# Swapping the two halves of a 128-token block for the expert dots: a pair of DMAs in place of identity matmuls

## The reference

```python
def reference(x_prompt, x_sample, ...):
    # for the prompt, then (with states and caches) for the samples
    q, k, v, g, qs, ks, vs = split(rms_norm(x, norm1_g) @ w_in)     # 2816 columns
    o_ret = retention(rotate(q), rotate(k), v)                      # 4 heads of 128, blocks of 128 tokens
    o_swa = sliding_window_attention(qs, ks, vs, sinks)             # 8 heads of 64, window 128
    h = x + concat(norm(o_ret) * silu(g), o_swa) @ w_out
    x2 = rms_norm(h, norm2_g)                                       # 128 tokens x 1024 in a block
    y = rms_norm(h + peer(x2), final_g)

def peer(xt):
    q = (xt @ peer_w_q).reshape(t, 8, 2, 128)
    s = einsum('thcd,hcnd->thcn', q, peer_sub_keys)                 # 16 x 128 scores of a token
    sv, si = top_k(s, 16)
    best, sel = top_k(sums of the 16 x 16 pairs, 16)                # 8 heads x 16 = 128 experts a token
    gates = softmax(best)
    hid = einsum('thkd,td->thk', peer_u[idx], xt)                   # dot of each expert row with the token
    return einsum('thk,thkd->td', gelu(hid) * gates, peer_v[idx])
```

## Time and profile before

| what | us |
|---|---|
| median of 3 runs | 3132.75 (3130.27 to 3137.91) |
| the profiled execution's own time | 3137.91 |
| its span, first to last instruction | 3136.1 |
| TensorE busy in the span | 2284.0 (73%) |
| VectorE busy | 2032.7 (65%) |
| GpSimd busy | 1172.1 (37%) |
| ScalarE busy | 1030.0 (33%) |
| gathers' share of the 16 DMA engines | 83.6% (1082.20 MB of 1213.13 MB) |
| mean granted clock of TensorE | 0.845 |

### The profile page before, as it was taken

The page is one execution under the profiler, slowest core; times in us unless marked ns, Lnnn a source line. Parts: engine busy times, 40 slices in busy tenths (PEclk is TensorE's granted clock), DMA queues, the critical chain, the costliest instruction groups (busy, mean ns, idle before and its releaser), DMA issues.

```text
span 3136.1 us, 29180 instructions
## 1 busy us (share of the span) xinstructions
PE 2284.0 (73%) x8830; PEld 981.5 (31%) x8830; DVE 2032.7 (65%) x4948; ACT 1030.0 (33%) x3292; POOL 1172.1 (37%) x1052
## 2 busy tenths in 40 slices
PE   7889859886798884757586577756785678568555
PEld 5668514552255421232221132212221222111111
DVE  3273546775478654668558865797569756966864
ACT  3312422334232432313432353325323343233221
POOL 0011434333443342324344444444444444444542
PEclk9999979998899877867898788878897799778777
DMA  8467999999999996979999999999999999999996
GB/s 313 149 225 282 427 418 407 415 419 422 421 413 418 417 420 275 370 290 401 423 421 404 410 422 421 421 409 409 421 416 416 411 414 410 421 390 422 421 421 270
DMA packets 201486, 1213.13 MB, mean 387 GB/s; under 512 B 25400, under 2 KB 52304, under 8 KB 67056
## 3 DMA queue, kind: packets, MB, share of 16 engines
q0 software_dynamic: 148608, 1082.20, 83.6%
q1 hardware_dynamic: 52720, 129.08, 11.2%
HBM read 1189.26 MB, written 21.54 MB: 386 GB/s over the span
## 4 chain that ended last, share of the span: by engine, by line
DMA 38%; PE 33%; DVE 11%; issue 5%; SPq 5%; ACT 4%; POOL 3%; another core or an unknown queue 0%; POOLq 0%; DVEq 0%; ACTq 0%
DMA ring<-in_peer_uv,idxg 34%; PE ps L886 13%; PE ps L855 7%; PE ps L637 6%; DVE ring L1580 6%; SPq L405 3%; POOL ring L563 3%; ACT ring L957 2%; DMA proj_scratch<-wo 1%; SPq L399 1%; DMA wo<-in_w_in 1%; PE ps L653 1%; PE ps L836 1%; PE ps L612 1%; DVE proj L1496 1%
## 5 line engine op out<-in xcount | busy, mean ns | idle before, releaser
L563 POOL DMA_INDIRECT ring<-in_peer_uv,idxg x1024 | 1159.1, 1132 | 1702.8 <-PE ps L886 1459.3
L886 PE MATMUL ps<-ring 128*64 128x512 f32 x4096 | 1236.8, 736 | 644.1 <-ACT ring L957 641.5
L1580 DVE SCALAR_TENSOR_TENSOR ring<-ring,xlo 128x1024 f32<-128x1024 f32 x512 | 626.3, 1223 | 535.0 <-DMA ring<-in_peer_uv,idxg 524.8
L1580 DVE SCALAR_TENSOR_TENSOR ring<-ring,xhi 128x1024 f32<-128x1024 f32 x512 | 626.6, 1224 | 378.1 <-DMA ring<-in_peer_uv,idxg 370.7
L886 PEld LDWEIGHTS ps<-ring 128*64 128x64 f32 x4096 | 289.4, 157 | 1440.1 <-ACT ring L957 964.3
L1127 ACT ACTIVATE small<-small 128x2 f32<-128x2 f32 x512 | 104.0, 203 | 1655.2 <-DVE ring L1580 1637.2
L637 PE MATMUL ps<-wo 128*128 128x176 f32 x1792 | 308.3, 331 | 51.2 <-issue 24.5
L637 PEld LDWEIGHTS ps<-wo 128*128 128x128 f32 x1792 | 285.8, 201 | 108.3 <-issue 79.9
L957 ACT ACTIVATE ring<-gdiag,small 128x64 f32<-128x64 f32 x1024 | 300.3, 340 | 16.8
L957 ACT ACTIVATE gdiag<-fold,gateg 128x64 f32<-128x64 f32 x1024 | 292.8, 333 | 1.5
L855 PE MATMUL ps<-keyw,work 128*128 128x512 f32 (+1 forms) x576 | 268.8, 612 | 1.1 <-ACT work L957 1.1
(11 more groups left out here) (200 smaller groups left out, 1564.4 us busy)
## 6 DMA issues: line engine op xcount, KB each, us to landing
wo<-in_w_in SPq DMA_DIRECT2D x48, 704.0 KB
ring<-in_peer_uv,idxg POOLq DMA_INDIRECT x1024
wo<-in_w_out SPq DMA_DIRECT2D x4, 4096.0 KB, 16.9
ring<-in_w_in SPq DMA_DIRECT2D x8, 1408.0 KB, 7.5
proj_scratch<-wo SPq DMA_DIRECT2D x112, 88.0 KB
proj<-proj_scratch SPq DMA_DIRECT2D x7, 1408.0 KB
ring<-in_wqT SPq DMA_DIRECT2D x16, 512.0 KB, 4.0
h<-in_x_prompt SPq DMA_DIRECT2D x10, 512.0 KB
```

The costliest lines, as they stand in the source:

```text
L563: nc.gpsimd.indirect_dma_start(row[r], None, A["peer_uv"], bass.IndirectOffsetOnAxis(ap=experts, axis=0)).then_inc(ld_row[r], 16)
L886: mm = nc.tensor.matmul(acc[side * HP:(side + 1) * HP, n * 512:(n + 1) * 512], row_u[r][:, 0:HP], row_v[r][:, n * 512:(n + 1) * 512], star ...
L1580: ins = stt(row_u[r], row_u[r], 1.0, (xlo, xhi)[unit % 2][:], ALU.mult, ALU.mult, accum_out=dot[:, r:r + 1])
```

## The change

The swapped halves are no longer made by TensorE. SyncE gets a new step, `move_tokens`: once the last score matmul of a block is done (`sc_mm`), so that `xT` is free, two DMAs copy the lower 64 partitions of `x2` to the upper 64 of `xT`, and the upper 64 to the lower, 256 KB each, both counting on `x2_moved`. The step stands behind `late(b, 84)`, and for block 0 behind the last load of the query weights. TensorE's swap at tick 89 goes, and with it the waits for `x2_taken` that protected its PSUM banks. `take_over` waits for `x2_moved` and reads the swapped halves from `xT` in SBUF in place of PSUM.

```diff
+            def move_tokens(b):
+
+                sp.wait_ge(sc_mm, b * 4 + 4)
+                sp.dma_start(xT[HP:P, :], x2[0:HP, :]).then_inc(x2_moved, 16)
+                sp.dma_start(xT[0:HP, :], x2[HP:P, :]).then_inc(x2_moved, 16)
...
             for n in range(12, NHC):
                 load_wqT(n)
+            move_tokens(0)
...
                 load_residual(b + 1)
+                late(b, 84)
+                move_tokens(b + 1)
                 late(b, 104)
                 move_picks(b + 1, 0)
...
                 pe.wait_ge(sc_out, 8)
-                pe.wait_ge(x2_taken, 4)
...
             def mixing(b):
                 yield 11
-                if b:
-                    pe.wait_ge(x2_taken, b)
...
-                if rows == P:
-                    yield at + 44
-                    pe.wait_ge(sc_out, b * 2 + 1)
-                    for n in range(2):
-                        for side in range(2):
-                            mm = nc.tensor.matmul(F[n][side * HP:(side + 1) * HP, :], ident[:, (1 - side) * HP:(2 - side) * HP],
-                                                  x2[:, n * 512:(n + 1) * 512], start=True, stop=True)
-                    mm.then_inc(x2_swapped, 1)
...
-                v.wait_ge(x2_swapped, b + 1)
+                v.wait_ge(x2_moved, b * 32 + 32)
                 me.did(nc.vector.tensor_copy(xlo[0:HP, :], x2[0:HP, :]))
                 me.did(nc.vector.tensor_copy(xhi[HP:P, :], x2[HP:P, :]))
-                me.did(nc.vector.tensor_copy(xlo[HP:P, :], FF(0, 2)[HP:P, :]))
-                me.did(nc.vector.tensor_copy(xhi[0:HP, :], FF(0, 2)[0:HP, :]))
+                me.did(nc.vector.tensor_copy(xlo[HP:P, :], xT[HP:P, :]))
+                me.did(nc.vector.tensor_copy(xhi[0:HP, :], xT[0:HP, :]))
```

More of the change, by code:

```diff
@@ L297, in build @@
         idx_taken, acc_out = sem("idx_taken"), sem("acc_out")
-        gates_taken, x2_swapped, x2_taken = sem("gates_taken"), sem("x2_swapped"), sem("x2_taken")
+        gates_taken, x2_moved, x2_taken = sem("gates_taken"), sem("x2_moved"), sem("x2_taken")
         moved = [sem("moved0"), sem("moved1")]
```

## The result

| kernel | median of runs, us | over before | 95% interval |
|---|---|---|---|
| before | 3131.52 (3129.15 to 3137.91) | 1 | |
| changed | 3153.21 (3147.04 to 3164.68) | 1.0063 | 1.0046 to 1.0081 |

The change makes the kernel 0.6% slower, some 20 us. The forecast was no change, 3129 us, with a range up to 3145; the time lies outside of it.

A forecast was written before the change was run, and what follows sets the result against it. Late blocks were taken as bound by DMA at 420 GB/s, block 0's front by TensorE's chain. -1.9 (front) - 6.6 (boundaries) + 4.9 (moves) = -3.6 us gave 3129 us on the median's scale, range 3120 to 3145.

The forecast's parts named there:

- the price of the six moves: Behind the scores of six blocks: 1.25 us per 512 KB at full rate, 7.5 in all, taken as 4.9 us.
- the room behind the scores: In windows where the scores end, lost DMA time could absorb 5.2 of the moves' 7.5 us.
- The rival of half rate: Each move through half the paths costs 2.5 us of gather time, 15 in all: about 3142 us, chance 0.22.
- both of its signs: Signs of half rate: windows behind the scores below 360 GB/s at share 1, late blocks of 332 us or more.
- block 0's front: On TensorE's chain from scores to late pieces, the missing swap saves 1.87 us, taken as 1.9.
- The boundaries' 6.6 us: At seven block boundaries take_over gets 1.07 us shorter, saving time where DMA was dry: 6.6 us together.
- The waits: VectorE's wait for x2_moved, the dropped x2_taken waits and SyncE's new wait hold nobody up: costed at nothing.
- the move in the sample stage: SyncE issues it after the stores at 1357.26 us, when just 130 GB/s flow: costed at nothing.
- TensorE's relief: Rival: TensorE bounds the fronts of blocks 1 to 3, so the swap saves 5.6 us more: 3121, chance 0.14.
- GpSimd's lockout by SBUF copies: Beside take_over's four SBUF copies the next gather could get some 0.4 us longer: nothing put in the sum.
- The sample stage: In the third block, with the sample tokens, the long waits on SyncE's queue were assumed unmoved.

The follow-up runs named there:

- the kernel without the moves: The changed kernel without its two DMAs per block, take_over waiting for the last score matmul instead: 3130.02 us, ratio 0.9994 to before.
- five kernels: The changed kernel and four variants of it, all moving 512 KB a block in DMAs of one half: late blocks of 333.0 to 333.3 us.
- short copies alone: The kernel before, swap matmuls included, with take_over's third and fourth copies reading stale xT in SBUF in place of PSUM: 3131.39 us, ratio 0.9998.
- the late: The changed kernel with both DMAs issued only after the dots of unit 112 of 128, for blocks 1 to 7: 3155.0 us, ratio 1.0076 to before.
- the pieces: The changed kernel with each block's swap in four pairs of DMAs of 256 columns, spread over the block: 3153.04 us, ratio 1.0071 to before.
- 128-partition one: The changed kernel with one 512 KB DMA over all 128 partitions in place of two between halves: 3137.68 us, ratio 1.0019 to before.
- lower 64: The changed kernel with one 256 KB DMA a block, partitions 0 to 63 of x2 to the same of xT: 3140.61 us, ratio 1.0032 to before.
- half of the bytes: The changed kernel with both DMAs moving only the first 512 of 1024 columns, 256 KB a block: 3140.31 us, ratio 1.0027 to before.
- both in their half: The changed kernel with two 64-partition DMAs that each stay in their half, same bytes and place: 3148.45 us, ratio 1.0067 to before.
- matmuls kept: The changed kernel with its DMAs and TensorE's swap matmuls also kept, their result unread: 3148.25 us, ratio 1.0072 to before.
- middle 64: The changed kernel with one 256 KB DMA a block, partitions 32 to 95 of x2 to the same of xT: 3135.94 us, ratio 1.0014 to before.

## Why the prediction was wrong

*The step that failed is the price of the six moves.* It stood at 1.25 us each at full rate, less the room behind the scores: 4.9 us in all, at most 7.5. Measured, the moves cost 3153.2 - 3130.0 = 23 us, 3.3 us for each of the seven later blocks. For one DMA over 128 partitions the term's upper end would have been right: 3137.7 - 3130.0 = 7.7 (by the intervals of the ratios some 4 to 12), where the prediction had 7.5 as the upper end and took 4.9. What it left out of its sum is that a DMA within one half of the partitions runs at about half the rate. The prediction had this as a rival and gave it 0.22. The Trainium skill states this rule on the page "SBUF — State Buffer", section "Door 1: The DMA port swizzle": 64 partitions of one half reach 8 of 16 ports, with about 218 GB/s. The trace agrees on the rates, 202 to 231 GB/s for moves of one half that run alone and 369 to 389 for those that reach both halves; the ports themselves no run here shows.

*The rival of half rate* had both of its signs right, late blocks of 332 us or more (333.3) and windows behind the scores below 360 GB/s at share 1 (321 to 329; in the kernel without the moves such windows read 356 at the least, at share 0.96). Its time, 3142, was still too low, for two reasons. It counted on 6.6 us from the boundaries; without these, and with the gain in block 0's front, it reads 3131.5 - 1.9 + 15 = 3144.6, or 3147 with seven moves in place of six. And it priced a move at 2.5 us, where a late block pays 3.4. Where this last 0.9 us goes is open: it isn't the place, the pieces or the crossing, since five kernels that differ in these agree within 0.3 us.

The medians of these five kernels lie further apart, 3148 to 3155. Their profiles, one each, differ most in block 2, which lasts 413 us in one and 429 in another. In the profile of the changed kernel the store of block 1's result took 17.7 us to land there,

```profile
1029.10 17.71 DMA out<-work
```

VectorE waited 7.55 us for it,

```profile
1046.98 1.43 DVE L1254 TENSOR_TENSOR work<-proj,qsT 128x256 f32<-128x256 f32 x4 [7.55 <-DMA out<-work]
```

and DMA ran at 169 GB/s for the 10 us from 1054. Moves aren't needed for this wait: the profile of short copies alone, which has none, shows 2.46 us of it, and of the kernels with moves the late, the pieces and the 128-partition one show 8.9 to 9.5, the lower 64 4.6, and the other four (half of the bytes, both in their half, matmuls kept, middle 64) none. What decides whether it comes is open.

*The room behind the scores* was no room. By bytes 5.2 us of transfers seemed to fit in the earlier trace rows, by DMA share nothing, and the prediction took the middle. The 128-partition DMA cost 7.7 us, with all seven at full price 1.25 x 7 = 8.8, and 1.4 us a block in the late blocks; so the share column was nearly right, as far as one such kernel shows.

*The boundaries' 6.6 us* were the second failed step. The copies did get 1.07 us shorter, and in the windows read behind a boundary more flowed (375 against 345 GB/s, 411 against 390). But in a block whose DMA engines are full for 326 of 330 us, by the prediction's own reading, such a gain was given back a few units later. The term was reckoned from the chain of waits at one place; the experiment with short copies alone puts it at 0.6 us (ratio 0.9998, and by its interval between 3.4 us faster and 2.2 slower).

*Block 0's front*, 1.9 us: right in mechanism. The swap's 1.87 us are gone from the chain, and the version that changes block 0 alone is faster, by 3.2 us in the medians and 2 to 8 by the interval of the ratio. The 7.6 us seen in one pair of profiles are mostly scatter: over all kernels the first `take_over` begins between 232.7 and 244.5 us, at 235.8 in the short-copy kernel, which keeps the matmuls, and at 244.5 in the kernel with the middle 64, which has none.

*The waits* were right in the main: VectorE doesn't wait for `x2_moved`. Put at nothing, but not quite nothing, was the move in the sample stage: SyncE's load of states (L421) was issued 3.8 us after the store at 1357.26 before, and 5.4 us after that store now, with the two moves in between. *TensorE's relief*, nothing in the sum, fits: its rival wanted 14 us from the front, the boundaries and the swap together (8.5 + 5.6), and the kernel without moves gained 4.7 at most. That GpSimd's lockout by SBUF copies needn't be in the sum was right too. In the late block of the changed kernel, the gather that begins beside the four copies is longer than the one ahead of it,

```profile
2454.97 0.94 POOL L572 DMA_INDIRECT ring<-in_peer_uv,idxg  x1 [0.88 <-PE ps L884]
2456.21 1.26 POOL L572 DMA_INDIRECT ring<-in_peer_uv,idxg  x1 [0.30 <-issue]
```

but the time with short copies alone is unchanged, with twice as many such copies. The twelve gathers that overlap these copies in this profile took 0.96 to 1.48 us; the seven beside PSUM copies only, in the profile of before, took 0.93 to 0.94.

*The sample stage*, assumed unmoved: its block 2 is 9 us longer in this profile, but it is 428 us long in this one, the late and the pieces kernel and 413 to 414 in three others with moves, against 419 before. So these profiles don't show that the moves lengthen it.

## What to carry to other kernels

Where the DMA engines are full, ask of each new transfer how many partitions of each half it touches, not only its bytes: a move from 64 partitions to the other 64 cost here about 2.5 to 3 times what the same bytes cost over all 128 (3.4 against 1.4 us in a late block, 23 against 8 in all). Don't count on room in a window in which the engines' share is 1, even if the bytes per second are low. And time gained at one stall of a kernel that is bound by transfers isn't gained until a change of that stall alone has been timed.

## What the runs showed of the hardware

A DMA from SBUF to SBUF that lies in partitions 0 to 63 moves 222 GB/s when it is alone, with all 16 engines busy (share 1.04); two of them, one in each half and issued one after the other, move 202 together at share 1.01. One of equal size on partitions 32 to 95 moves 369 GB/s at share 0.90, and one over all 128 moves 389 at 0.95. So a busy share of 1 doesn't mean the full rate. That the engines hold each other up at the shared paths would explain it; the share alone doesn't show it.
